# A four-sublayer streaming encoder step in three-part fp32 products: the third role's rounding placed behind the second's

## The reference

```python
def swiglu(x, w_gate, w_up, w_down):
    return (jax.nn.silu(x @ w_gate) * (x @ w_up)) @ w_down
...
for l in range(DEPTH):                       # DEPTH = 2
    if l == N_A_LAYERS:                      # shared keys, values, forget gates
        kv = rms_norm(x, g_kv_b) @ w_kv_b ...
    x = x + 0.5 * swiglu(rms_norm(x, g_norm[l, 0]), ...)
    # l = 0: differential attention, l = 1: forgetting attention
    x = x + o @ w_o
    x = x + 0.5 * swiglu(rms_norm(x, g_norm[l, 2]), ...)
y = rms_norm(x, g_final)
```

## Time and profile before

| | |
|---|---|
| times of three runs | 2512.48, 2517.8, 2520.25 us, median 2517.8 |
| profiled execution | 2516.2 us, its span 2514.0 us |
| busy share of the span | PE 96%, DVE 74%, ACT 53%, POOL 22% |
| mean granted PE clock | 0.992 |

### The profile page before, as it was taken

The page is one execution under the profiler, slowest core; times in us unless marked ns, Lnnn a source line. Parts: engine busy times, 40 slices in busy tenths (PEclk is TensorE's granted clock), DMA queues, the critical chain, the costliest instruction groups (busy, mean ns, idle before and its releaser), DMA issues. The chain is left out here.

```text
span 2514.0 us, 48940 instructions
## 1 busy us (share of the span) xinstructions
PE 2413.0 (96%) x18377; PEld 2267.6 (90%) x18377; DVE 1859.1 (74%) x3710; ACT 1338.0 (53%) x2870; POOL 546.1 (22%) x421
## 2 busy tenths in 40 slices
PE   8899999999998999999999999999999999999998
PEld 7899999788678999999988889999996699999998
DVE  7887979422687888787935889787928878787865
ACT  6555556201785655555622555555618856555554
POOL 0222122344000122222135122222131001222210
PEclk9999999999999999999999999999999999999999
DMA  5656565232763465756434665666457644666652
GB/s 133 122 116 139 108 139 105 88 117 85 282 241 108 93 122 112 141 119 133 94 84 138 172 130 111 138 125 129 99 210 255 224 117 78 138 116 138 124 112 82
DMA packets 419397, 334.20 MB, mean 133 GB/s; under 512 B 20641, under 2 KB 379738, under 8 KB 418914
## 3 DMA queue, kind: packets, MB, share of 16 engines
q1 hardware_dynamic: 279376, 246.98, 31.8%
q0 software_dynamic: 133136, 65.82, 21.4%
q10 hardware_dynamic: 6658, 18.37, 2.0%
HBM read 314.98 MB, written 16.13 MB: 132 GB/s over the span
## 5 line engine op out<-in xcount | busy, mean ns | idle before, releaser
L925 PE MATMUL PS<-x_area,w_area 128*128 128x320 f32 x3096 | 482.2, 309 | 0.0
L925 PEld LDWEIGHTS PS<-x_area,w_area 128*128 128x128 f32 x3096 | 461.1, 188 | 0.3 <-DVE w_area L2276 0.3
L2276 DVE TENSOR_TENSOR w_area<-R,w_area 128x512 fp32r<-128x512 f32 (+2 forms) x583 | 357.1, 617 | 119.1 <-ACT w_area L1638 118.3
L1638 ACT ACTIVATE w_area<-R 128x512 fp32r<-128x512 f32 (+2 forms) x583 | 324.8, 567 | 223.3 <-PE PS L925 88.6
L2276 DVE TENSOR_TENSOR r_area<-R,r_area 128x512 fp32r<-128x512 f32 (+2 forms) x437 | 270.6, 620 | 115.4 <-ACT r_area L1638 105.0
L925 PE MATMUL PS<-r_area,w_area 128*128 128x320 f32 x1584 | 271.2, 314 | 25.1 <-ACT PS L1723 17.1
L1638 ACT ACTIVATE r_area<-R 128x512 fp32r<-128x512 f32 (+2 forms) x437 | 248.0, 568 | 60.6 <-DVE R L2297 40.2
L925 PEld LDWEIGHTS PS<-r_area,w_area 128*128 128x128 f32 x1584 | 243.1, 191 | 32.9 <-ACT PS L1723 29.8
L1723 ACT ACTIVATE PS<-PS 128x320 f32<-128x320 f32 x438 | 179.8, 417 | 160.0 <-PE PS L925 143.7
L1148 PE MATMUL PS<-w_area,xn_hi 128*128 128x512 f32 x800 | 252.4, 397 | 4.9 <-POOL w_area L769 3.6
L925 PE MATMUL PS<-r_area 128*128 128x320 f32 x1392 | 238.4, 311 | 8.4 <-ACT PS L1723 6.0
(11 more groups left out here) (341 smaller groups left out, 4169.6 us busy)
## 6 DMA issues: line engine op xcount, KB each, us to landing
R<-in_w_ffn_up_dram SPq DMA_DIRECT2D x45, 512.0 KB, 5.3
R<-in_w_ffn_gate_dram SPq DMA_DIRECT2D x43, 512.0 KB, 5.4
R<-in_w_ffn_up_dram SPq DMA_DIRECT2D x86, 256.0 KB, 3.7
R<-in_w_ffn_up_dram POOLq DMA_DIRECT2D x86, 256.0 KB, 4.7
R<-in_w_ffn_gate_dram SPq DMA_DIRECT2D x82, 256.0 KB, 4.6
R<-in_w_ffn_gate_dram POOLq DMA_DIRECT2D x81, 256.0 KB, 4.9
R<-in_w_ffn_down_dram SPq DMA_DIRECT2D x52, 384.0 KB, 3.8
R<-in_w_ffn_down_dram SPq DMA_DIRECT2D x88, 192.0 KB, 3.2
```

What stands on the lines that cost most here:

```text
L925: last = pe.matmul(PS[:, bank, 0:HT], a[:, k, :], b, start=(start and opens), stop=(k == n - 1 and a is lo), skip_group_check=True)
L1638: act.activation(role_parts(f, g, s, role)[0], role_source(f, g, s, role), ACT.Copy).then_inc(sem("early_cast") if key in EARLY_COUNT else ...
L2276: dve.tensor_tensor(lo, role_source(f, g, s, role), hi.bitcast(F32), ALU.subtract).then_inc(sem("early_split") if key in EARLY_COUNT else ...
```

## The change

Six edits, one diff:

1. In `splits`, in DVE's `ffn_sets` and `opening_down`, and in ACT's, role S3 of the present set moves from behind S4 of the present set to behind S2 of the next. PE's order stays as it was.
2. In ACT's `opening_down`, copy 1 is put ahead of the rounding of hidden part 5, and copy 2 ahead of the roundings of S4, hidden part 4, S1 and S2.
3. SP issues the S1 block of the next set ahead of the two other pieces of the present one.
4. At the seams (qkv, kv, qb), the first tiles are loaded as soon as their place is free, and the finishing of column tile 5 moves behind the rounding of seam tile 0.
5. In the first block, the roundings and low parts of the first hidden pair move behind the first set.
6. The store of the turned keys is issued behind the first set of block 2 and has a semaphore of its own.

```diff
@@ splits
-        out += ([(then, "W11")] if then else []) + [(at, "S4")] + ([(at, "S3")] if at != order[0] else [])
-        out += ([(then, "S1"), (then, "S2")] if then else []) + [(at, "W22")] + ([(then, "W12")] if then else [])
+        out += ([(then, "W11")] if then else []) + [(at, "S4")] + ([(then, "S1"), (then, "S2")] if then else [])
+        out += ([(at, "S3")] if at != order[0] else []) + [(at, "W22")] + ([(then, "W12")] if then else [])
@@ SP: load_ffn
-                for g, s in chain(f):
-                    if set_at(f, g, s) is not early:
-                        quarter_load(f, g, s)
+                first_quarter(*sets[0])
+                for key, then in zip(sets, sets[1:] + [None]):
+                    if then is not None:
+                        first_quarter(*then)
+                    other_quarters(*key)
@@ ACT: opening_down
                 hidden_rows(f, *prev, "1")
+                copy_rows(f, *cur, 1)
                 hidden_rows(f, *prev, "5")
-                copy_rows(f, *cur, 1)
                 hidden_rows(f, *prev, "7")
                 hidden_rows(f, *prev, "2")
                 role_high(f, *then, "W11")
+                copy_rows(f, *cur, 2)
                 role_high(f, *cur, "S4")
                 hidden_rows(f, *prev, "4")
+                role_high(f, *then, "S1")
+                role_high(f, *then, "S2")
                 role_high(f, *cur, "S3")
-                role_high(f, *then, "S1")
-                copy_rows(f, *cur, 2)
-                role_high(f, *then, "S2")
                 role_high(f, *cur, "W22")
@@ ACT: ffn_sets
                     if n:
                         rows_on(f, *prev, 0)
-                        role_high(f, *cur, "S3")
...
                     if then is not None:
                         role_high(f, *then, "S2")
+                    if n:
+                        role_high(f, *cur, "S3")
                     role_high(f, *cur, "W22")
...
+                    if n == 0 and after_first is not None:
+                        after_first()
@@ DVE: opening_down
                 hidden_lows(f, *prev, "4")
-                role_low(f, *cur, "S3")
                 dve.wait_ge(w_split, SPLIT[(f, *cur, "S4")])
                 role_sum(f, *then, "S2")
                 role_low(f, *then, "S1")
                 role_low(f, *then, "S2")
                 fifth_rows(f, *cur)
+                role_low(f, *cur, "S3")
                 role_low(f, *cur, "W22")
@@ DVE: ffn_sets
                     if turned:
                         hidden_sums(f, *prev, ("5", "7", "6"))
-                    if n:
-                        role_low(f, *cur, "S3")
...
                     if turned:
                         hidden_sums(f, *prev, ("4",))
                         hidden_lows(f, *prev, "7")
+                    if n:
+                        role_low(f, *cur, "S3")
                     role_low(f, *cur, "W22")
@@ DVE and ACT: ffn (the seams)
                     tile_low(name, 0)
+                    finish_one(KB - 3)
                     sums_out(f, *last)
@@ ACT: the key store of block 2
-            act.wait_ge(sem("heads_read"), 30)
-            act.dma_start(k_scr, ...).then_inc(stored, 16)
-            ffn(2, None, partial(finish_tile, 2, 3, 2, 4), "qb")
+            def store_keys():
+                act.wait_ge(sem("heads_read"), 30)
+                act.dma_start(k_scr, ...).then_inc(sem("kt_stored"), 16)
+            ffn(2, None, partial(finish_tile, 2, 3, 2, 4), "qb", store_keys)
```

More of the change, by code:

```diff
@@ L590, in set_load, with first_quarter @@
                                  weight_rows(f, g, s, part)).then_inc(landed, 16)
-            def quarter_load(f, g, s):
-                key, p = (f, g, s), LOAD[f, g, s] % 2
+            def first_quarter(f, g, s):
+                key = f, g, s
                 if PLAN.raw_free[key, 3]:
@@ L599, in quarter_load, with other_quarters @@
                 sp.dma_start(role_source(*key, "S1"), weight_block(*key, 0, 1)).then_inc(w_loaded3, 16)
+            def other_quarters(f, g, s):
+                key, p = (f, g, s), LOAD[f, g, s] % 2
                 if PLAN.raw_free[key, 1]:
@@ L618, in load_ffn @@
                     load_constants()
-                for g, s in chain(f):
-                    if set_at(f, g, s) is not early:
-                        quarter_load(f, g, s)
+                sets = [(f, *at) for at in chain(f) if set_at(f, *at) is not early]
+                first_quarter(*sets[0])
[3 more added lines that the diff above has]
+                    other_quarters(*key)
                 for g in range(len(GROUPS)):
@@ L635, in load_square @@
                 base, s, first = BASE[name], SLOT[name], 0
-                if free is not None:
+                if free is None:
+                    first = 1
+                    for u in range(2):
+                        opening_tile(name, u, *cols(w, (s + u) % 2, u * P))
+                else:
                     first = 2
@@ L650, in load_square, with opening_tile, row_tile, load_opening_rows @@
                     tile(base + m * 2 + 1, 1 - s, *cols(w, 1 - s, m * 2 * P + P))
-            def load_rows(w, base, par, n_tiles, first=0):
-                with sp.Fori(0, n_tiles) as n:
+            def opening_tile(name, j, view, src):
+                sp.wait_ge(w_split, PLAN.raw_free[name, j])
+                sp.dma_start(view, src).then_inc(w_loaded[LOAD[name, j] % 2], 16)
+            def row_tile(w, s, u, at):
+                return (raw[s][:, 0:1024].rearrange("p (k m) -> p k m", k=2),
+                        w[u * 256:(u + 1) * 256, bass.ds(at, 512)].rearrange("(k p) m -> p k m", p=P))
+            def load_opening_rows(w, name, column):
+                for u in range(4):
+                    opening_tile(name, u, *row_tile(w, (SLOT[name] + u) % 2, u, column * 512))
+            def load_rows(w, base, par, n_tiles, first=0, done=0):
+                with sp.Fori(done, n_tiles) as n:
                     for u in range(4):
                         s = (par + u) % 2
-                        tile(base + n * 4 + u, s, raw[s][:, 0:1024].rearrange("p (k m) -> p k m", k=2),
-                             w[u * 256:(u + 1) * 256, bass.ds(n * 512 + first * 512, 512)].rearrange("(k p) m -> p k m", p=P))
+                        tile(base + n * 4 + u, s, *row_tile(w, s, u, n * 512 + first * 512))
             def load_attention(x, vc, f_scr):
@@ L1842, in ffn_sets, with ffn @@
                         finish_one(tiles)
-                        finish_one(tiles + 1)
+                        if then is not None:
+                            finish_one(tiles + 1)
                 copy_rows(f, *order[-1], 3)
-            def ffn(f, mean=None, finish_one=None, name=None):
-                ffn_sets(f, mean, finish_one)
+            def ffn(f, mean=None, finish_one=None, name=None, after_first=None):
+                ffn_sets(f, mean, finish_one, after_first)
                 if name is not None:
-                    for k in range(2):
-                        tile_high(name, k)
-                        finish_one(KB - 2 + k)
+                    tile_high(name, 0)
+                    finish_one(KB - 3)
+                    tile_high(name, 1)
+                    for k in range(KB - 2, KB):
+                        finish_one(k)
                     return
@@ L2125, in _, with first_hidden_casts @@
             x_highs("4")
-            for part in HIDDEN_PARTS[1:]:
-                first_hidden_cast(part)
-            ffn(0, None, partial(finish_tile, 0, 0, 0, 1), "qkv")
+            def first_hidden_casts():
+                for part in HIDDEN_PARTS[1:]:
+                    first_hidden_cast(part)
+            ffn(0, None, partial(finish_tile, 0, 0, 0, 1), "qkv", first_hidden_casts)
             act.wait_ge(w_used, BASE["qkv"])
@@ L2166, in _ @@
             act.wait_ge(step, count.next())
-            act.activation(lf1, lf2, ACT.Ln, bias=1.0).then_inc(sem("ln_ready"), 1)
+            act.activation(lf1, lf2, ACT.Ln, bias=1.0).then_inc(sem("small_exps"), 1)
             act.wait_ge(sem("rows_read"), 8 * TB + 2)
@@ L2240, in _ @@
                 y_out(n)
-            act.wait_ge(stored, STORED["kt"])
+            act.wait_ge(stored, STORED["bv"])
         @block.vector
@@ L2633, in ffn_sets, with ffn @@
                         finish_one(tiles)
-                        finish_one(tiles + 1)
-            def ffn(f, root, event, version, g_next, name=None):
+                        if then is not None:
+                            finish_one(tiles + 1)
+            def ffn(f, root, event, version, g_next, name=None, after_first=None):
                 def finish_one(k):
```

48 lines of the change are left out of this document (26 added, 22 removed).

## The result

| | before | after |
|---|---|---|
| median (lowest to highest), four runs each | 2518.2 us (2512.5 to 2520.3) | 2781.3 us (2776.7 to 2790.5) |
| span of the profiled execution | 2514.0 us | 2788.5 us |
| PE stands still, all gaps of its timeline over 0.15 us | 93.1 us | 264.9 us |
| PE busy | 2413.0 us | 2514.4 us |
| mean granted clock | 0.992 | 0.951 |

The account below looks back on a forecast made before the run. The prediction took PE, busy 96% of the span, as the bound: 2516.2 us + 152.5 for the late S3 - 4 for the other edits + 46 for the clock = 2710.7, so 2711 us (7.7% slower), range 2630 to 2780.

Parts of the forecast that it names:

- turned sets: 25 sets where PE would stand 3.3 us each ahead of S3, waiting for DVE's low S3: 82.5 us.
- openings: 15 openings where low S3, and PE with it, would come 2.4 us later each: 36 us.
- down sets of 3-pair groups: 30 down sets with a next set, where PE would stand about 0.8 us each ahead of S3: 24 us.
- 2-pair groups' down sets, gate sets behind them: Four 2-pair groups at 2 us net each, 8 us; gate sets behind a down set, some 2 us in all.
- seams, hidden pair, all else: Edits other than late S3: seams gain 3 us, hidden pair 1, loads and key store nothing; together -4 us.
- clock: PE's matmuls at 1.2 GHz behind the new gaps of turned sets and openings: 46 us, ends 0 and 68.
- The replay of DVE's rows: DVE's profile rows replayed in the new order: low S3 in a turned set ends at 146.4, PE stands 3.3 us.
- If two thirds (27) cost 1.7 us: Clock price: 27 of the 40 gaps in turned sets and openings lose 1.7 us each, 46 us.
- Rival 3: W11 loads wait for the later split of S3, missing by 2 us per turned set: 50 us more, 2761 us; chance 0.11.
- PE waits for no load in these sets: Reason for costing at nothing the S1 block's load one step sooner, ahead of W11.
- wins nothing: Openings: DVE's low S3, not copy 2, released PE at S3, so an earlier copy 2 gains 0 us.
- up to 0.9 more: Openings: copy 2, now ahead of the cast of S4, must wait for PE's S2, possibly costing up to 0.9 us.

Follow-up runs that it names:

- e2: Kernel before with only the move of S3 behind S2 of the next set (table of splits, DVE, ACT): 2751.8 us, ratio 1.093.
- e5: Changed kernel with filler multiplications on PE behind the wait for copy 2, 12 per turned set and 16 per opening; part of the values is replaced: 2713.5 us, 1.079.
- e6: Changed kernel with the load order of before, the present set's other pieces asked for ahead of the next set's S1 block: 2769.2 us, ratio 1.102.
- e13: Kernel before with only the new load order, the next set's S1 block ahead of the present set's other pieces: 2650.0 us, ratio 1.053.
- e10: Kernel before with only the early copies 1 and 2 of the openings: 2536.7 us, ratio 1.008.
- e8: Changed kernel with S3 in its old place and the old load order, keeping early copies, seams, hidden pair and key store: 2533.4 us, ratio 1.008.
- e11: Kernel before with only the seams' tiles, the first hidden pair's work and the key store changed: 2511.7 us, ratio 0.998.
- e1: Changed kernel with S3 back in its old place, the five other edits kept: 2654.6 us, ratio 1.056.
- e7: Changed kernel with the key store back ahead of block 2's first set: 2783.0 us, ratio 1.107.

## Why the prediction was wrong, point by point

By spans the forecast was +194.5 us (152.5 - 4 + 46), and it came to +274.5. Where the 80 us between them lie, in us over the kernel before, from the gaps of PE's timeline and its busy time; the sums differ by roundings:

| term | forecast | edit 1 alone (e2) | changed kernel |
|---|---|---|---|
| turned sets | 82.5 | 78.8 | 78.6 |
| openings | 36 | 28.4 | 39.6 |
| down sets of 3-pair groups | 24 | 26.5 | 26.6 |
| 2-pair groups' down sets, gate sets behind them | 8 + 2 | 16.4 | 17.3 |
| second sets of the four blocks | 0 | 4.7 | 20.4 |
| seams, hidden pair, all else | -4 | 0.4 | -10.6 |
| pauses under 0.15 us | 0 | 0 | 1.3 |
| clock | 46 | 81.8 | 101.4 |
| sum | 194.5 | 237.0 | 274.5 |

Two steps failed. The clock was priced at 46 us, and it cost 82 with edit 1 alone and 101 in the changed kernel. And the other five edits, put at -4 us, cost 27 (263 less 236). The waits that the main edit makes came as forecast, 155 us for 152.5, though not each of its terms did, and the signs named for them are there: the gaps in turned sets, openings and down sets, and low S3 directly ahead of low W22.

- **S3 behind S2 of the next set.** The replay of DVE's rows held: 3.14 us for 3.3, 0.65 and 0.89 us in the steady down sets for 0.73 and 0.93 (in blocks 1 to 3 single ones reach 2.2). In an opening of a 3-pair group the gap ahead of S3 grows from 1.15 to 3.56 us in e2, 2.4 as forecast; the 0.42 us ahead of S2 go, so that the openings as a whole came to less. The 2-pair groups and the gate sets behind them cost 16 us in place of 10. All other edits aside, this one alone gives +236 us (e2).
- **The clock.** "If two thirds (27) cost 1.7 us" is the step that failed most. Of the 25 turned sets 20 fell to the lower level, 13 at about 1.7 us and 7 at 2.9 or 3.0; of the 15 openings all fell, most at 2.2 to 3.0. That sums to 82 us over these 40 gaps (77 in e2), and e5 gives 65 to 75 by another way. The other 20 us or so are elsewhere, behind second sets and 2-pair down sets among others (3.1 us behind the 12.51 us gap, 3.0 behind one of 4.00), and were not forecast at all. I had taken the price from two gaps of before and the share from one that had not fallen. The trace of before had a dearer one as well, which I did not use: the 10 us behind the 2.40 us gap at 644.26 had 0.72. The Trainium skill (page "TensorE: Matmul & The Clock Gate", section "Part 1: The HAM clock gate (the "warmup" mystery)") says that an array that idled runs at the lower clock until it has been busy for a while. That every one of these gaps then pays was my strict reading of it, not its words; at 35 of 40 it came nearer than my two thirds.
- **The load order costed at nothing.** Rival 3 had late W11 loads, but for another reason, the later split of S3. What the runs show is that the load stood in SP's queue behind the next set's S1 block. In turned sets behind a late S3 it costs nothing (their gaps are 3.14 us with the old load order of e6 too); it shows in the second sets of blocks 1 to 3, 13 us together. Its price in this kernel is 9 to 12 us (e6). Its price as an edit of its own is 133 (e13), which "PE waits for no load in these sets" could not see: the cover was ACT's, not PE's.
- **The early copies.** For the earlier copy 2 I had said "wins nothing" and "up to 0.9 more", and set this off against an earlier start of DVE. It costs 0.56 us in each 3-pair opening and 0.6 in the others, with and without the late S3, and the clock with it: alone 20 us (e10). In the changed kernel it is not hidden: e6, which is e2 with the copies, the seams, the hidden pair and the key store, takes 17 us more than e2, and the same edits without the late S3 take 18 (e8).
- **Seams, hidden pair, key store.** -4.5 us alone (e11) for -4. The wait at 59.03 went from 3.66 to 0.83 us, and 4.54 us came at 72.87, in the next set, where I had said that this work would hold PE about as long.
- **Which effects add.** Late S3 +236, early copies +20 and the rest -4.5 make 252, and e6, which has them all, measured +254: these add. The load order does not. It costs 133 alone, 121 beside the early copies and the rest (e1 less e8), and 9 to 12 beside the late S3, which already makes PE wait longer at the same places. So all together is +263 and not the 385 that the single prices make.

## What to carry to other kernels

Where PE is the bound and each part of its input has a deadline, a part that is wanted sooner must be made sooner: replaying the helper engines' rows in the new order gave the gaps of turned sets, steady down sets and (with the copies left alone) 3-pair openings to within 0.2 us. Price loads by what stands behind them in their queue and by the waits of the engine that casts them, not by PE's waits. And look at what the clock adds to a new gap on PE: the 40 here were 3.4 us long in the mean and brought 2.0 us at the lower clock each, though only 35 of them did, at 1.5 to 3.0 us.

## What the runs showed of the hardware

- A gap of 3.13 or 3.14 us costs nothing, 1.7 or 2.9 us of clock at places with the same instructions (1200.05, 1170.50 and 1035.45 above). The length of the gap alone doesn't decide it, and nor does the place: behind the gap of 1035.45, which lost 2.9 us, e7 lost nothing (its gap at 1036.59, clock 1.00), and behind that of 318.95, which lost nothing, it lost 3.0 (its gap at 315.83, clock 0.70).
- The eleven gaps of 1.15 us in the openings of before cost no clock. At 1.70 to 1.73 us, in e10, seven of eleven did, six of them 1.6 or 1.7 us and one 3.0, and e10's PE is busy for 2429.2 us against 2413.0 with the same matmuls. So the half microsecond of waiting that e10 has more came with up to five times as much at the lower clock. (The small gap ahead of it has changed too, from 0.42 or more to 0.58 or more and to a later place, so the length of the one gap is not shown to be the cause.)
- Small multiplications inside the gaps kept the granted clock at 1.00 behind all 40 of them (e5) and brought back 75 us of 2788 in the profiled executions, 65 by the medians. Here the waits should go instead, but where a gap can't be closed they are worth a try.
